# A hybrid layer's scan: decays and their scaling placed first in each projection tile

## The chip, the cores and the metric

The kernel runs on one core of one Trainium2 chip. The metric is the device time of one execution in microseconds (us). Three runs of the kernel before gave 2807.34 to 2811.86 us, with a median of 2810.05 us.

## The reference, cut to what matters

Two transformer-like blocks run one after the other on 512 tokens of width 1024. The first block has a state-space scan, a windowed attention and a mixture of experts; the second has attention and dense feed-forward layers. The change touches only the scan of the first block and what shares its time:

```python
z, xbc, dt_raw, q, k, v, g_ssd, g_att = jnp.split(h @ w_in, IN_SPLITS, axis=-1)
...
a_cum = jnp.cumsum(dt_c * a.reshape(G, J), axis=2)            # G=4 groups, J=8 heads, chunks of L=128
seg = a_cum[:, :, :, None] - a_cum[:, :, None, :]
decay = jnp.exp(jnp.where(causal, seg, -jnp.inf))
cb = jnp.einsum('bclgn,bcsgn->bclsg', cm, bm)
y_diag = jnp.einsum('bclsgj,bcsgjp->bclgjp', cb[..., None] * decay, xdt)
states = jnp.einsum('bclgn,bclgjp->bcgjpn', bm, xdt * decay_to_end[..., None])
...                                                            # carried over the 4 chunks
y_off = jnp.einsum('bclgn,bcgjpn->bclgjp', cm, prev) * jnp.exp(a_cum)[..., None]
y = y_diag + y_off + xs * d_skip
...
q = partial_rope(rms_norm(q, q_norm_g), cos, sin)              # the same for k; v is only projected
```

Everything is float32; the large products split each operand in a high and a low part and use three matmuls.

## The kernel before, in words

Each stage of the kernel has one function for each engine (`qkv_pe`, `qkv_act`, `qkv_dve`, `qkv_pool`, `qkv_sp`, and `mix_*` in the same way). A function lists its engine's instructions in program order. An engine takes them strictly in that order, and they wait for one another across engines by semaphores. So where a call stands in such a function decides behind which waits it sits.

**The stage qkv** is a loop over 14 tiles t: two of k, eight of q (each 128 columns of the weights, 24 matmuls of 512 columns on TensorE, "dense") and four of v (24 matmuls of 256 columns). For the q and k tiles ScalarE copies and squares the product (L1035, L1036), TensorE sums the squares of tile t-1 (L1025, "blk"), ScalarE makes the root from them (L1044, L1046), VectorE scales (L1066, "normed"). Then comes the rotation of tile t-2: TensorE (L1019, "rot"), VectorE times the sine (L1058), GpSimd times the cosine (L1082), VectorE adds them (L1061). VectorE copies the v tiles (L1070). Weight pieces are split ahead of use, the high part on ScalarE (`piece_hi`, L415) and the low part on VectorE (`piece_lo`, L429).

**The scan** has 16 units i, one for each of 4 groups and 4 chunks c (c = i mod 4). Unit i is laid beside tile t = i + 4 (`S_FIRST` = 4), the later ones beside the rounds of the next stage. For one unit:

- `decay_sp`: SyncE loads the unit's 512 KB of cumulated decays, broadcast from DRAM, in one of two buffers (the ring `EX`, L842). The load of unit i waits until the products of unit i-2 have left the buffer.
- `decay_act`: ScalarE, in place, eight Relu instructions (L888) and one Exp over 1024 columns (L890).
- `cb_pe`, `cb_dve`: TensorE makes C·B (L849), VectorE masks it (L897).
- `weights_dve`: VectorE multiplies the 1024 columns of decays by it (L903, "weights").
- `scan_pool`: GpSimd makes x·dt (L941, "xd"), x·dt·decay-to-end (L947, "xe") and x·D (L948, "skip").
- `scan_pe`: TensorE multiplies weights and xd (L861, 16 matmul records, "ydiag"), the old state (L871, "yoff", not for c = 0) and the new state (L879, "state", not for c = 3).
- `scan_dve`: VectorE adds them to y and carries the state (L911 to L933).

In tile t the products of unit t-5 run on TensorE, behind the tile's dense. On VectorE the weights of unit t-5 stand at the head of tile t, behind the piece; on ScalarE the decays of unit t-4 stand at the end of tile t, behind the norms of tile t-1.

**The stage mix** walks one list, `MIX`, on all engines: 19 rounds r, in each the scan step "s0" of unit r+10 (decays, C·B) and "s1" of unit r+9 (the products), four attention steps ("a2", "a1", "b0", "a0"), two z tiles ("z": 24 matmuls of 256 columns, ScalarE tanh L1229, VectorE L1273, GpSimd L1294), and the weight pieces of z ("w"). The scan is through after round 6. In mix the weights of unit r+9 are the first thing of "s0" on VectorE, behind the z steps of the round before. The raw z pieces have a single buffer, so that the load of a piece waits until the piece ahead is split.

Of the kernel before, what the change touches and what calls it, by code (L numbers as in the profile page):

```python
# [220 lines left out]
def build(nc, d, out):  # L221
    ctx = ExitStack()
    with ctx:
# [753 lines left out]

        def qkv_pe(e):
            for t in range(14):
                if 1 < t < 10:  # L980
                    qkv_dense(e, t)
                elif t >= 10:
# [12 lines left out]
                    m.then_inc(*(WS1.of(ns[0]).free(K.pe, "mm", t) if t == 13 else K.pe.up("mm", t)))  # L995
                    if t == 13:
                        WS1.of(ns[1]).frees.update(WS1.of(ns[0]).frees)
                if t == S_FIRST:
                    e.wait_ge(*X.act.to("turned", 19))
                    e.wait_ge(*D.act.to("done"))  # L1000
                if t >= S_FIRST:
                    cb_pe(e, t - S_FIRST)
                if t > S_FIRST:
                    scan_pe(e, t - 1 - S_FIRST)
                if 0 <= t - 4 < 2:
# [21 lines left out]
        def qkv_act(e):  # L1027
            for t in range(14):
                piece_hi(e, qkv_ahead(t))
                if t < 10:  # L1030
                    b, q = BR.of("qkv", t), HBQ.take(t)
                    for s, n in q.before:
                        e.wait_ge(s, n)
                    e.wait_ge(*K.pe.to("mm", t))
                    e.activation(qkv_out(t), b.ap[:, :], ACT.Copy).then_inc(*K.act.up("cp", t))  # L1035
                    e.activation(q.ap, b.ap[:, :], ACT.Square).then_inc(*b.free(K.act, "sq", t))  # L1036
                if 0 <= t - 4 < 2:
                    b = BR.of("swap", t - 4)
                    e.wait_ge(*K.pe.to("swap", t - 4))
                    e.activation(KT[:, 2 * (t - 4) + 1, :], b.ap[:, :], ACT.Copy).then_inc(*b.free(K.act, "swap", t - 4))  # L1040
                if 0 <= t - 1 < 10:
                    b, q = BR.of("blk", t - 1), HBQ.of(t - 1)
                    e.wait_ge(*K.pe.to("blk", t - 1))
                    e.activation(q.ap, b.ap[:, :], ACT.Ln, bias=C["eps"]).then_inc(*b.free(K.act))  # L1044
                    e.wait_ge(*K.act.now())
                    e.activation(q.ap, q.ap, ACT.Exp, scale=-0.5).then_inc(*K.act.up("rs", t - 1))  # L1046
                if t >= S_FIRST:
                    decay_act(e, t - S_FIRST)

        def qkv_dve(e):  # L1050
            for t in range(14):
                piece_lo(e, qkv_ahead(t), False)
                if t > S_FIRST:
                    weights_dve(e, t - 1 - S_FIRST)
                if 0 <= t - 2 < 10:
                    b, x, q = BR.of("rot", t - 2), qkv_out(t - 2), HBQ.of(t - 2)
                    e.wait_ge(*K.pe.to("rot", t - 2))
# [9 lines left out]
                if t >= 10:  # L1067
                    b = BR.of("qkv", t)
                    e.wait_ge(*K.pe.to("mm", t))
                    e.tensor_copy(VT[:, t - 10, :], b.ap[:, 0:256]).then_inc(*b.free(K.dve, "v", t))  # L1070
                if t >= S_FIRST:
                    cb_dve(e, t - S_FIRST)
                if t > S_FIRST:
                    scan_dve(e, t - 1 - S_FIRST)

        def qkv_pool(e):
            e.wait_ge(*L.act.to("cos"))
# [28 lines left out]
        for r in range(19):  # L1106
            first = [j // 4 for j in Z_ROUNDS[r] if j % 4 == 0]
            MIX += [("w", AT["z", a, 1]) for a in first]
            MIX += [(f, r + S_BESIDE - lag) for f, lag in (("s0", 0), ("s1", 1)) if r + S_BESIDE - lag < 16]
            MIX += [(f, r - lag) for f, lag in (("a2", 3), ("a1", 2), ("b0", 1), ("a0", 0)) if 0 <= r - lag < 16]  # L1110
            MIX += [("z", j) for j in Z_ROUNDS[r]]
            MIX += [("w", AT["z", a, 1] + 1) for a in first]

# [117 lines left out]
        def mix_dve(e):  # L1231
            for what, i in MIX:
                if what == "s0":
                    weights_dve(e, i - 1)
                    cb_dve(e, i)
                if what == "s1":
                    if i == 15:
                        weights_dve(e, i)
                    scan_dve(e, i)
                if what == "a0":  # L1240
                    n_, kv = ATT_UNITS[i]
                    w = 256 if n_ else 128
# [2359 lines left out]
```

## Time and profile before

| | |
|---|---|
| median of three runs | 2810.05 us |
| the profiled execution | 2808.63 us, with a span of 2806.8 us |
| span outside its first and last instruction | 1.83 us |
| TensorE busy in the whole span | 92% |
| tiles 5 to 13 of qkv, up to the last ydiag | 214.5 to 354.3 us |
| rounds 0 to 6 of mix (the rest of the scan) | 354.3 to 484.0 us |

The span is what the profile's rows are counted in. Busy TensorE is not TensorE at its peak: its clock has two levels, 2.4 and 1.2 GHz, and a row of a stretch gives the granted share as PEclk.

### The profile page before, as it was taken

Reading aid. Unit: us, or ns where it says so; the run is one execution under the profiler, and the core shown is the slowest. Engines: PE = TensorE matmul, PEld = TensorE weight load, DVE = VectorE, ACT = ScalarE, POOL = GpSimd, SP = SyncE. Lnnn points to the kernel's source line nnn. Section 1 sums busy time; section 2 is a strip of 40 time slices with the busy share of each in tenths; the row PEclk is TensorE's granted clock in tenths of the full one; section 3 lists DMA queues with packets and bytes.
Section 4 is the critical chain, followed back from the end, with each engine's and each line's share of the span. In section 5 each row is a group of like instructions: output and inputs, shape, how many; then the busy total and the mean of one; then the engine's idle time right before and its main releaser. Section 6 shows DMA issues by size and latency. Waiting matters only on the chain.

```text
span 2806.8 us, 41459 instructions
## 1 busy us (share of the span) xinstructions
PE 2585.2 (92%) x16510; PEld 2114.5 (75%) x16510; DVE 1145.8 (41%) x2009; ACT 1055.8 (38%) x2157; POOL 826.5 (29%) x538
## 2 busy tenths in 40 slices
PE   7998778999997888888999998999999999999999
PEld 6875556888875555555798878999999887777877
DVE  7754444533124111111435664134257776512212
ACT  4444343553222211112435564323324555532231
POOL 1002343422331032200221103655541111465553
PEclk9998778999998999999999999999999999999999
DMA  4231121233328999999331111233332111233332
GB/s 144 83 86 45 43 70 46 61 106 83 99 71 321 409 426 426 426 426 419 138 106 50 57 31 53 83 91 98 91 87 76 49 46 46 60 90 91 105 91 67
DMA packets 328417, 378.78 MB, mean 135 GB/s; under 512 B 10480, under 2 KB 300400, under 8 KB 303648
## 3 DMA queue, kind: packets, MB, share of 16 engines
q1 hardware_dynamic: 327072, 371.91, 38.3%
q0 software_dynamic: 1152, 4.19, 0.4%
q8 instruction: 134, 2.20, 0.3%
q14 instruction: 59, 0.48, 0.1%
HBM read 371.81 MB, written 4.26 MB: 134 GB/s over the span
## 4 chain that ended last, share of the span: by engine, by line
PE 64%; DMA 12%; DVE 9%; issue 6%; ACT 5%; POOL 5%; SPq 0%; ACTq 0%; DVEq 0%; POOLq 0%
DMA early<-in_w_up_e 11%; PE bank L2478 5%; PE bank L2480 5%; PE bank L2479 5%; PE bank L1972 5%; PE bank L2985 4%; PE bank L2986 4%; PE bank L2987 4%; PE bank L443 3%; PE bank L444 3%; PE bank L445 3%; POOL split L2453 2%; DVE early L684 2%; PE bank L861 1%; PE bank L1186 1%
## 5 line engine op out<-in xcount | busy, mean ns | idle before, releaser
L2453 POOL TENSOR_TENSOR split<-keep,split 128x1024 fp32r<-128x1024 f32 x143 | 348.8, 2443 | 453.0 <-ACT split L2427 453.0
L2478 PE MATMUL bank<-x_hi,split 128*128 128x264 f32 (+1 forms) x1280 | 397.6, 311 | 11.1 <-POOL split L2453 9.3
L2480 PE MATMUL bank<-x_hi,split 128*128 128x264 f32 (+1 forms) x1280 | 390.6, 305 | 0.0
L2479 PE MATMUL bank<-x_lo,split 128*128 128x264 f32 (+1 forms) x1280 | 390.4, 305 | 0.0
L2427 ACT ACTIVATE split<-keep 128x1024 fp32r<-128x1024 f32 x192 | 200.2, 1050 | 222.8 <-PE bank L2987 208.0
L1972 PE MATMUL bank<-early 128*64 128x256 f32 x2048 | 236.5, 384 | 40.0 <-DMA early<-in_w_up_e 32.1
L2478 PEld LDWEIGHTS bank<-x_hi,split 128*128 128x128 f32 x1280 | 241.4, 189 | 32.3 <-issue 19.8
L1972 PEld LDWEIGHTS bank<-early 128*64 128x64 f32 x2048 | 165.7, 138 | 122.0 <-issue 72.4
L2479 PEld LDWEIGHTS bank<-x_lo,split 128*128 128x128 f32 x1280 | 241.6, 189 | 10.1 <-issue 0.2
L2480 PEld LDWEIGHTS bank<-x_hi,split 128*128 128x128 f32 x1280 | 240.6, 188 | 10.4
L3023 DVE TENSOR_TENSOR mlp<-mlp,bank 128x264 f32<-128x264 f32 (+1 forms) x96 | 49.5, 515 | 326.7 <-ACT mlp L3002 326.7
L2985 PE MATMUL bank<-hidden0h,split 128*128 128x264 f32 x512 | 145.5, 284 | 1.1 <-issue 1.1
L415 ACT ACTIVATE w_split<-early 128x1024 fp32r<-128x1024 f32 (+1 forms) x101 | 105.6, 1047 | 106.3 <-PE bank L445 97.0
L2986 PE MATMUL bank<-hidden0l,split 128*128 128x264 f32 x512 | 145.0, 283 | 0.0
L2987 PE MATMUL bank<-hidden0h,split 128*128 128x264 f32 x512 | 145.0, 283 | 0.0
L2090 DVE TENSOR_TENSOR early<-early,bank 128x256 f32<-128x256 f32 x32 | 13.5, 421 | 314.9 <-PE bank L2013 198.1
L1996 PE MATMUL bank<-early 128*64 128x512 f32 x512 | 116.9, 598 | 21.5 <-DVE early L2097 21.5
L3033 DVE TENSOR_TENSOR mlp<-bank,roots 128x264 f32<-128x264 f32 (+1 forms) x96 | 46.9, 516 | 206.1 <-PE bank L2987 206.1
L429 DVE TENSOR_TENSOR w_split<-early,w_split 128x1024 fp32r<-128x1024 f32 (+1 forms) x70 | 87.4, 1248 | 103.6 <-ACT w_split L415 103.6
L443 PE MATMUL bank<-x_hi,w_split 128*128 128x512 f32 x304 | 123.6, 407 | 1.0 <-DVE w_split L429 0.4
L3002 ACT ACTIVATE mlp<-bank 128x264 f32<-128x264 f32 (+1 forms) x96 | 43.5, 453 | 202.7 <-PE bank L2480 202.7
L445 PE MATMUL bank<-x_hi,w_split 128*128 128x512 f32 x304 | 119.1, 392 | 0.0
(490 smaller groups left out, 6132.9 us busy)
## 6 DMA issues: line engine op xcount, KB each, us to landing
early<-in_w_gate_e SPq DMA_DIRECT2D x64, 1024.0 KB, 11.2
early<-in_w_up_e SPq DMA_DIRECT2D x64, 1024.0 KB, 11.4
early<-in_w_down_e SPq DMA_DIRECT2D x64, 1024.0 KB, 10.7
early<-in_w_in SPq DMA_DIRECT2D x68, 512.0 KB, 3.7
keep<-in_mlp_w_in SPq DMA_DIRECT2D x64, 512.0 KB, 3.9
keep<-in_mlp_w_out SPq DMA_DIRECT2D x64, 512.0 KB, 3.7
keep<-in_a_w_qkv SPq DMA_DIRECT2D x24, 512.0 KB, 4.6
early<-decay_rows SPq DMA_DIRECT2D x16, 512.0 KB, 5.8
```

The costliest lines, as they stand in the source:

```text
L443: e.matmul(o, hi[:, k, :], xh, start=first and k == 0, stop=False, skip_group_check=True)
L445: m = e.matmul(o, lo[:, k, :], xh, start=False, stop=last and k == 7, skip_group_check=True)
L1972: m = e.matmul(b.ap[cols(j, 64), o:o + 256], x.ap[:, k, cols(j, 64)], wtile(us[j], 8, 256)[:, k, :], start=k == 0, stop=k == 7, skip_group ...
L1996: m = e.matmul(b.ap[cols(j, 64), :], ht.ap[:, f * 128 + 64 * j:f * 128 + 64 * j + 64], wtile(us[j], 2, 1024)[:, f, cols(q, 512)], start=f ...
L2427: e.activation(hi, x, ACT.Copy).then_inc(*S.act.up("hi", n))
L2453: e.tensor_tensor(lo, x, whole(hi), ALU.subtract).then_inc(*u.free(sig_, "lo", n))
L2478: e.matmul(o, hi[:, k, :], xh, start=k == 0, stop=False, skip_group_check=True)
L2479: e.matmul(o, hi[:, k, :], xl, start=False, stop=False, skip_group_check=True)
L2480: m = e.matmul(o, lo[:, k, :], xh, start=False, stop=k == 7, skip_group_check=True)
L2985: e.matmul(o, hi[:, k, :], yh[:, k, n0 - at:n1 - at], start=k == 0, stop=False, skip_group_check=True)
L2986: e.matmul(o, hi[:, k, :], yl[:, k, n0 - at:n1 - at], start=False, stop=False, skip_group_check=True)
L2987: m = e.matmul(o, lo[:, k, :], yh[:, k, n0 - at:n1 - at], start=False, stop=k == 7, skip_group_check=True)
```

## The change: what it does

In the stage qkv, TensorE's C·B of unit t-4 moves from behind the dense of tile t ahead of it. ScalarE's decays of unit t-4 move from the end of tile t to behind its weight piece, ahead of the copy, the square and the root. On VectorE tile t now does, behind its weight piece, the mask and the weights of unit t-4 and then the additions of unit t-5, all ahead of rotation, norm and v copy; before, it did the weights of unit t-5 there, and mask and additions at the end. So weights are made in the tile ahead of their products. The stage mix gets an entry "sw": the weights of unit r+10 stand in round r behind "a0" and ahead of "z", where before they stood in round r+1 behind the z steps of round r and that round's first piece. No instruction is added or removed, and no load or buffer is changed.

```diff
--- before.py
+++ after.py
@@ -977,6 +977,11 @@
 
         def qkv_pe(e):
             for t in range(14):
+                if t == S_FIRST:
+                    e.wait_ge(*X.act.to("turned", 19))
+                    e.wait_ge(*D.act.to("done"))
+                if t >= S_FIRST:
+                    cb_pe(e, t - S_FIRST)
                 if 1 < t < 10:
                     qkv_dense(e, t)
                 elif t >= 10:
@@ -995,11 +1000,6 @@
                     m.then_inc(*(WS1.of(ns[0]).free(K.pe, "mm", t) if t == 13 else K.pe.up("mm", t)))
                     if t == 13:
                         WS1.of(ns[1]).frees.update(WS1.of(ns[0]).frees)
-                if t == S_FIRST:
-                    e.wait_ge(*X.act.to("turned", 19))
-                    e.wait_ge(*D.act.to("done"))
-                if t >= S_FIRST:
-                    cb_pe(e, t - S_FIRST)
                 if t > S_FIRST:
                     scan_pe(e, t - 1 - S_FIRST)
                 if 0 <= t - 4 < 2:
@@ -1027,6 +1027,8 @@
         def qkv_act(e):
             for t in range(14):
                 piece_hi(e, qkv_ahead(t))
+                if t >= S_FIRST:
+                    decay_act(e, t - S_FIRST)
                 if t < 10:
                     b, q = BR.of("qkv", t), HBQ.take(t)
                     for s, n in q.before:
@@ -1044,14 +1046,15 @@
                     e.activation(q.ap, b.ap[:, :], ACT.Ln, bias=C["eps"]).then_inc(*b.free(K.act))
                     e.wait_ge(*K.act.now())
                     e.activation(q.ap, q.ap, ACT.Exp, scale=-0.5).then_inc(*K.act.up("rs", t - 1))
-                if t >= S_FIRST:
-                    decay_act(e, t - S_FIRST)
 
         def qkv_dve(e):
             for t in range(14):
                 piece_lo(e, qkv_ahead(t), False)
+                if t >= S_FIRST:
+                    cb_dve(e, t - S_FIRST)
+                    weights_dve(e, t - S_FIRST)
                 if t > S_FIRST:
-                    weights_dve(e, t - 1 - S_FIRST)
+                    scan_dve(e, t - 1 - S_FIRST)
                 if 0 <= t - 2 < 10:
                     b, x, q = BR.of("rot", t - 2), qkv_out(t - 2), HBQ.of(t - 2)
                     e.wait_ge(*K.pe.to("rot", t - 2))
@@ -1068,10 +1071,6 @@
                     b = BR.of("qkv", t)
                     e.wait_ge(*K.pe.to("mm", t))
                     e.tensor_copy(VT[:, t - 10, :], b.ap[:, 0:256]).then_inc(*b.free(K.dve, "v", t))
-                if t >= S_FIRST:
-                    cb_dve(e, t - S_FIRST)
-                if t > S_FIRST:
-                    scan_dve(e, t - 1 - S_FIRST)
 
         def qkv_pool(e):
             e.wait_ge(*L.act.to("cos"))
@@ -1108,6 +1107,7 @@
             MIX += [("w", AT["z", a, 1]) for a in first]
             MIX += [(f, r + S_BESIDE - lag) for f, lag in (("s0", 0), ("s1", 1)) if r + S_BESIDE - lag < 16]
             MIX += [(f, r - lag) for f, lag in (("a2", 3), ("a1", 2), ("b0", 1), ("a0", 0)) if 0 <= r - lag < 16]
+            MIX += [("sw", r + S_BESIDE)] if r + S_BESIDE < 16 else []
             MIX += [("z", j) for j in Z_ROUNDS[r]]
             MIX += [("w", AT["z", a, 1] + 1) for a in first]
 
@@ -1231,12 +1231,11 @@
         def mix_dve(e):
             for what, i in MIX:
                 if what == "s0":
-                    weights_dve(e, i - 1)
                     cb_dve(e, i)
                 if what == "s1":
-                    if i == 15:
-                        weights_dve(e, i)
                     scan_dve(e, i)
+                if what == "sw":
+                    weights_dve(e, i)
                 if what == "a0":
                     n_, kv = ATT_UNITS[i]
                     w = 256 if n_ else 128
```

VectorE in the stage qkv, the kernel before, at one tile with c = 1 or 2 (L1058 is the sine product of rotation and so the first instruction behind the weights of unit t-5):

```order
L903 TENSOR_TENSOR early<-early 128x1024
L1058 TENSOR_TENSOR early<-bank,early 128x512
L1061 TENSOR_TENSOR early<-early 128x512
L1066 SCALAR_TENSOR_TENSOR early<-early,lasting 128x512
L897 TENSOR_TENSOR early<-bank,lasting 128x128
L911 TENSOR_TENSOR early<-early,bank 128x512
L917 TENSOR_TENSOR ints<-bank,early 128x512
L919 TENSOR_TENSOR early<-early,ints 128x512
L930 TENSOR_TENSOR early<-early 128x512
L933 TENSOR_TENSOR early<-early,bank 128x512
L429 TENSOR_TENSOR w_split<-early,w_split 128x1024
L903 TENSOR_TENSOR early<-early 128x1024
```

VectorE at the same place in the kernel of the change, whose lines L1061, L1064 and L1069 are L1058, L1061 and L1066 of before:

```order
L429 TENSOR_TENSOR w_split<-early,w_split 128x1024
L897 TENSOR_TENSOR early<-bank,lasting 128x128
L903 TENSOR_TENSOR early<-early 128x1024
L911 TENSOR_TENSOR early<-early,bank 128x512
L917 TENSOR_TENSOR ints<-bank,early 128x512
L919 TENSOR_TENSOR early<-early,ints 128x512
L930 TENSOR_TENSOR early<-early 128x512
L933 TENSOR_TENSOR early<-early,bank 128x512
L1061 TENSOR_TENSOR early<-bank,early 128x512
L1064 TENSOR_TENSOR early<-early 128x512
L1069 SCALAR_TENSOR_TENSOR early<-early,lasting 128x512
```

L903 now follows L897 of its own unit directly and stands ahead of the additions of the unit before; the rotation comes last.

ScalarE in the stage qkv, the kernel before, tiles of q (L1035 and L1036 copy and square, L1044 and L1046 make the root, L415 is the weight piece of the next tile):

```order
L1035 ACTIVATE early<-bank 128x512
L1036 ACTIVATE early<-bank 128x512
L1044 ACTIVATE early<-bank,lasting 128x512
L1046 ACTIVATE early<-early 128x512
L888 ACTIVATE early<-early 128x128 x8
L890 ACTIVATE early<-early 128x1024
L415 ACTIVATE w_split<-early 128x1024
```

ScalarE there in the kernel of the change, with L1037, L1038, L1046 and L1048 for the four lines:

```order
L415 ACTIVATE w_split<-early 128x1024
L888 ACTIVATE early<-early 128x128 x8
L890 ACTIVATE early<-early 128x1024
L1037 ACTIVATE early<-bank 128x512
L1038 ACTIVATE early<-bank 128x512
L1046 ACTIVATE early<-bank,lasting 128x512
L1048 ACTIVATE early<-early 128x512
```

The decays L888 and L890, which wait for their load, now stand ahead of the copy and the square, which wait for the dense.

VectorE in round 1 of mix, the kernel before (L1250 to L1263 are the attention step "a0", L1273 the two z steps, L903 the weights of the unit whose products run in the next round):

```order
L1250 SCALAR_TENSOR_TENSOR early<-bank,lasting 128x256 x2
L1254 TENSOR_REDUCE early<-early 128x4
L1260 TENSOR_TENSOR early<-early,lasting 128x4
L1262 TENSOR_TENSOR early<-lasting,early 128x4
L1263 TENSOR_SCALAR early<-early 128x4
L1273 SCALAR_TENSOR_TENSOR early<-early,bank 128x256 x2
L429 TENSOR_TENSOR w_split<-early,w_split 128x1024
L903 TENSOR_TENSOR early<-early 128x1024
```

The same in the kernel of the change (every line number but L903 and L429 is one less):

```order
L1249 SCALAR_TENSOR_TENSOR early<-bank,lasting 128x256 x2
L1253 TENSOR_REDUCE early<-early 128x4
L1259 TENSOR_TENSOR early<-early,lasting 128x4
L1261 TENSOR_TENSOR early<-lasting,early 128x4
L1262 TENSOR_SCALAR early<-early 128x4
L903 TENSOR_TENSOR early<-early 128x1024
L1272 SCALAR_TENSOR_TENSOR early<-early,bank 128x256 x2
L429 TENSOR_TENSOR w_split<-early,w_split 128x1024
```

L903 no longer stands behind the z steps and the weight piece.

## Rows read from the trace of the kernel before

**Rows 1.** Waits, 207 to 490 us: waiting, releaser, us in total, times, longest.

```profile
PE bank L861 <- DVE early L903: 54.8, 14, 11.7
```

**Rows 2.** Windows by stretch; columns as in the first row.

```profile
core 0: us, PE busy (x) PEld busy (x) DVE busy (x) ACT busy (x) POOL busy (x), PEclk, DMA share, GB/s
214.50:354.30 139.80, 108.32 (x435) 79.03 (x433) 66.03 (x81) 52.84 (x118) 40.99 (x33) 0.77 0.18 46
354.30:380.90 26.60, 14.91 (x83) 11.61 (x82) 9.56 (x17) 9.51 (x25) 9.41 (x8) 0.68 0.30 79
380.90:484.00 103.10, 85.60 (x504) 67.85 (x502) 49.38 (x97) 43.41 (x127) 39.03 (x33) 0.80 0.19 52
484.00:493.10 9.10, 9.10 (x75) 7.90 (x76) 4.06 (x11) 5.13 (x15) 5.65 (x4) 1.00 0.20 59
```

**Rows 3.** Timeline of PE, tile 7: start, duration, instruction, idle before and releaser.

```profile
248.87 0.79 PE L443 MATMUL bank<-x_hi,w_split 128*128 128x512 f32 x1
...
254.76 0.38 PE L849 MATMUL bank<-early 128*128 128x128 f32 x2
259.51 3.65 PE L861 MATMUL bank<-early 128*128 128x64 f32 x16 [4.37 <-DVE early L903]
...
267.18 0.80 PE L443 MATMUL bank<-x_hi,w_split 128*128 128x512 f32 x1
```

**Rows 4.** Timeline of PE, tile 3, which has no scan, and tile 13.

```profile
198.63 0.79 PE L443 MATMUL bank<-x_hi,w_split 128*128 128x512 f32 x1
...
204.52 1.02 PE L1019 MATMUL bank<-early,lasting 128*128 128x512 f32 x2
205.38 1.02 PE L1025 MATMUL bank<-early,lasting 128*128 128x512 f32 x2
205.83 0.79 PE L443 MATMUL bank<-x_hi,w_split 128*128 128x512 f32 x1
...
352.53 1.90 PE L861 MATMUL bank<-early 128*128 128x64 f32 x16
```

**Rows 5.** Timeline of DVE, tile 3 (first row) and tile 7.

```profile
207.75 0.69 DVE L1061 TENSOR_TENSOR early<-early 128x512 f32<-128x512 f32 x1 [1.48 <-POOL early L1082]
...
248.62 0.69 DVE L1058 TENSOR_TENSOR early<-bank,early 128x512 f32<-128x512 f32 x1 [8.09 <-PE bank L1019]
250.79 1.45 DVE L1061 TENSOR_TENSOR early<-early 128x512 f32<-128x512 f32 x1 [1.48 <-POOL early L1082]
252.16 1.53 DVE L1066 SCALAR_TENSOR_TENSOR early<-early,lasting 128x512 f32<-128x512 f32 x1
...
257.05 1.22 DVE L429 TENSOR_TENSOR w_split<-early,w_split 128x1024 fp32r<-128x1024 f32 x1
258.19 1.22 DVE L903 TENSOR_TENSOR early<-early 128x1024 f32<-128x1024 f32 x1
```

**Rows 6.** Timeline of ACT, tile 7: the decays of one unit.

```profile
250.74 2.44 ACT L888 ACTIVATE early<-early 128x128 f32<-128x128 f32 x8
253.21 1.06 ACT L890 ACTIVATE early<-early 128x1024 f32<-128x1024 f32 x1
```

**Rows 7.** All 16 decay loads, issue to landing.

```profile
DMA to landing us min/median/max: 5.5/5.8/8.1
```

**Rows 8.** Timeline of POOL: xd in tile 7.

```profile
250.65 1.03 POOL L941 TENSOR_TENSOR early<-early 128x512 f32<-128x512 f32 x1
```

**Rows 9.** Timeline, start of mix: POOL's z piece, DVE's z piece, z tiles on PE.

```profile
357.69 2.34 POOL L429 TENSOR_TENSOR w_split<-early,w_split 128x1024 fp32r<-128x1024 f32 x1
...
364.79 1.23 DVE L429 TENSOR_TENSOR w_split<-early,w_split 128x1024 fp32r<-128x1024 f32 x1 [8.62 <-ACT w_split L415]
...
375.03 0.39 PE L1186 MATMUL bank<-w_split,x_hi 128*128 128x256 f32 x1
...
380.89 0.39 PE L849 MATMUL bank<-early 128*128 128x128 f32 x2
```

**Rows 10.** Waits of SyncE's queue, 780 to 900 us.

```profile
SPq L1891 <- DVE lasting L1467: 40.5, 1, 40.5
```

## The prediction

> **What bounds the kernel now.** I read the waits between engines first, because busy shares say nothing about order. From 207 to 490 us TensorE waits 14 times, 54.8 us in all, and always with the same pair: the products of a scan unit (L861) wait for VectorE's weights (L903) [rows 1]. The windows then show how wide the matter is. From tile 5 to the last ydiag beside a projection tile pass 139.8 us, and up to the end of the scan another 26.6 and 103.1 us. TensorE has 60.7 us there with no matmul at all (139.8 - 108.3, 26.6 - 14.9 and 103.1 - 85.6 give 31.5 + 11.7 + 17.5), and its granted clock is 0.77, 0.68 and 0.80. In a round of mix without the scan it is busy all the time, at 1.00 [rows 2]. The other engines are busy at most half of these stretches [rows 2], so nothing but the order of work can hold TensorE up.
>
> The timeline of tile 7 shows the order. Its period is 267.18 - 248.87 = 18.3 us. Dense ends and C·B starts at 254.76; ydiag starts only at 259.51, 4.37 us idle, and then takes 3.65 us [rows 3], against 1.90 us in tile 13, where nothing had stalled [rows 4]. So a stall is paid twice: once as the wait, and once because TensorE then runs at its lower level, 1.2 GHz, for what follows. The tile before the scan begins shows the unstalled price: dense, rot and blk in 205.83 - 198.63 = 7.20 us [rows 4].
>
> VectorE's timeline of the same tile says why the weights are late. It runs without a pause from the sine at 248.62 to the end of the weights at 258.19 + 1.22 = 259.4, but for 1.48 us in which GpSimd multiplies the cosine. That is 10.8 us [rows 5]. It starts only when TensorE has done rot, and dense, beside which it runs, takes less than 6 us (204.52 - 198.63) [rows 4]. The weights stand last in this chain although their inputs have long been there: ScalarE's decays ended at 253.21 + 1.06 = 254.3 [rows 6].
>
> **The change, part by part.** No instruction comes or goes, so the sum is one of waits.
>
> *Stage qkv, TensorE alone.* A 512-column float32 product costs 205.38 - 204.52 = 0.86 us at full clock [rows 4], C·B about 0.3 [rows 3] and ydiag 1.9 [rows 4]. A tile with c = 1 or 2 then costs 7.20 + 0.3 + 1.9 + 2 x 0.86 = 11.1 us, one with c = 0 or 3 (no yoff, or no state) 10.3. A v tile is shorter by 24 x (0.227 - 0.122) = 2.5 us; the 0.122 is half a z pair over 24, (380.89 - 375.03)/48 [rows 9], the 0.227 is (204.52 - 198.63 - 0.43)/24 [rows 4], where 0.43 is my reading of the start. Tiles 5 to 9 (tile 5 has the 0.86 of a swap instead of yoff): 3 x 11.1 + 2 x 10.3 = 53.9. Tile 10: 8.6; tile 11, with no blk, 7.7; tile 12, with no rot and c = 3, 6.5; tile 13 up to the end of ydiag 5.6. Sum 82.3 us, against 139.8.
>
> *What the new order makes it wait for.* Let T be the end of the ydiag of unit i-2. The decay load of unit i is issued then and lands 5.8 us later, 8.1 at worst [rows 7]. ScalarE takes 2.44 + 1.06, some 3.5 us [rows 6], and VectorE 1.2 for the weights [rows 5]: T + 10.5. Behind that now stand the additions of unit i-1 (from 253.6 to 257.05, 3.4 us), the sine (0.7), GpSimd's cosine (1.5) [rows 5] and xd (1.03) [rows 8], which ydiag of unit i needs: T + 17.2, and ydiag ends at T + 19.1. That is two tiles, so 9.6 us a tile: less than TensorE's 11.1, and TensorE does not wait. VectorE's own tile stays 10.8 us long [rows 5], also below 11.1. Moving ScalarE's decays ahead of copy and square costs them T + 9.3, about when dense ends (T + 9.2), and what needs the square stands a tile later; I take 0. With the load at 8.1 us the chain gives 10.7 a tile: still 0. C·B ahead of dense waits for a bank that the mask of the unit before frees a tile earlier; its worth is 0.
>
> In the v tiles TensorE's 7 to 8 us fall below the chain's 9.6. Tiles 11 and 12 then stall some 2 to 3 us each and pay the lower clock: I take 6 us for both together, with 0 and 12 as bounds. Stage qkv: 82.3 + 6 = 88, so **-52 us**.
>
> A rule of the Trainium skill speaks against the move. What the rows show is this: VectorE's addition of two SBUF operands takes 0.69 us with GpSimd idle and 1.45 us with GpSimd running its scan operations [rows 5]. The Trainium skill, page "SBUF — State Buffer", section "Who interferes with whom", says that a VectorE instruction with two SBUF inputs and a GpSimd one that reads SBUF lock each other out, whichever comes second waiting. By that rule, the trace agrees, the piece and the weights can each be lengthened when GpSimd's skip overlaps them; by the rule at its worst the sum would be smaller by 1.2 us in each of nine tiles. By the rows alone a doubled L903 would make VectorE's tile 12.0 us, 0.9 over TensorE's; I take 0 and keep nine times 0.9 = 8 us for the range.
>
> *Start of mix.* Let E be the end of the last ydiag, 354.3 now. z tile 0 starts at 375.03, E + 20.7. It stood behind the products of unit 9, whose weights stood behind the z piece that VectorE ended at 364.79 + 1.23 = 366.0, E + 11.7. That piece hangs on the single raw buffer, which GpSimd frees at 357.69 + 2.34 [rows 9], and the change does not touch it. Weights 9 now stand ahead of it, so the products run while the piece is awaited and z starts at about E + 11.8: -8.9 us. It starts after an idle stretch, so I add 3.5 us for a z pair partly at the lower clock (an estimate: 5.86 us at full clock [rows 9], 11.7 if all of it were at half, and somewhat over the middle of the two). Together **-5.4 us**.
>
> *Rounds 1 to 6 of mix.* Now 103.1 us, 17.2 each [rows 2]. A round without the scan takes 9.1 us at full clock and with the whole attention [rows 2]; the scan adds 0.3 + 1.9 + 1.7 = 3.9. A z pair and the scan alone give 9.8; all of it 13.0. The attention joins step by step in these rounds, so I take 11.1, 67 us; bounds 59 and 78. In VectorE's list the weights now fill the time in which it waited for ScalarE's exp and tanh. So **-36 us**, bounds -44 and -25.
>
> *After the scan* nothing changes, and the gain has to survive. The next place where loads bound the kernel is the experts' weights; their first load waits 40.5 us in SyncE's queue for a VectorE instruction of the stage before [rows 10]. So it starts with the compute and moves with it: the gain is kept.
>
> Sum: 52 + 5.4 + 36 = 93 us. The profiled execution took 2808.6 us, 1.4 below the median of the runs; 2808.6 - 93 = 2715.6, on the median's scale 2717. The sum lets every stall be gone to the last tenth; I give back 3 us for that: **2720 us**.
>
> **The rivals.**
> *A, the stall gets shorter but stays* (chance 0.22). What speaks for it: VectorE's 10.8 and TensorE's 11.1 us are close, and after each longer wait the clock falls. If in each of 15 tiles and rounds about 1.5 us of wait and 1.5 us of lower clock remain, 45 us are lost: 2765 us. Against it: the same stretch shows waits to be harmful above all when VectorE's whole chain stands between rot and ydiag [rows 3, 5], and that chain is cut.
> *B, the gain is absorbed later* (0.03). If the expert loads bounded the time from an issue that does not move, all but some us would be lost, and the time would be 2800 to 2810. [Rows 10] speak against it.
> *C, slower* (0.04). The decays now stand ahead of the copy on ScalarE, and their load is issued only after a ydiag. If the load comes so late that the square is not there a tile later, blk waits, the root and the norm with it, and then rot, and ydiag behind them. From T the square has to be done by the blk of the next tile, about T + 20; load, decays and copy give T + 10.5 [rows 6, 7]. It decides from a landing of 15 us on. For a loss against before, a tile must be above 17 us, so the landing must be at 22 us; at 24 us it would be 2 us a tile over 9 tiles, 2830 us. The slowest of 16 took 8.1 us [rows 7].
> *The forecast* has 0.71.
>
> A rule of the Trainium skill bears on rival A. First the row: after 4.37 us idle ydiag runs at the lower level, 3.65 instead of 1.90 us [rows 3, 4]. The page "TensorE: Matmul & The Clock Gate", section "Part 1: The HAM clock gate (the "warmup" mystery)", describes the same two levels, with the lower one as the state after idleness.
>
> **How the numbers follow.** The bounds of the forecast are 0 or 12 us for the v tiles, up to 8 us in the q tiles, 59 to 78 in the rounds, and none of the 3 us given back: 2720 - 6 - 8 - 3 = 2703 to 2720 + 6 + 8 + 11 = 2745 us. Rival A adds the part up to its 2765. Leaving out its upper half, B and C, about 2 in 10, the range is 2700 to 2757. A measurement of this kernel can tell 0.2%, 5.6 us, from no change. The forecast, A and most of what lies between give faster 0.94; half of B same, 0.02; C and the unknown slower 0.04.
>
> **What the profile after would show.** The waits of L861 for L903 are gone or below 10 us. TensorE's period is 11 us in tiles 6 to 9, and ydiag takes 1.9 us there. PEclk is near 1.00 up to tile 10. The v tiles 11 and 12 show ydiag waiting for GpSimd's xd. z tile 0 starts some 12 us after the last ydiag beside a tile. Rounds 1 to 6 take 10 to 13 us, and a round without the scan 9.1 as before. I am wrong if the rotation, now last on VectorE, makes rot or xd the new wait in every tile, or if the clock stays low with short waits.

## The result and the profile after

| | before | changed |
|---|---|---|
| median, side by side | 2809.81 us | 2717.55 us (2715.61 to 2721.07, 4 runs) |
| ratio, 95% interval | | 0.9673 [0.9657, 0.9690] |
| profiled execution, its span | 2808.63, 2806.8 us | 2717.27, 2715.5 us |
| granted clock of TensorE, whole span | 0.967 | 0.985 |

The forecast was 2720 us, range 2700 to 2757. Two single runs further on, one of 3172 us in experiment 3 and one of 3599 us with the first edit of experiment 4, lie far above the others of their kernels, with a granted clock of 0.75 and 0.65, and are left out of the ratios.

I read the profile after in the order of the views before. First TensorE's waits from 200 to 410 us (which engine and line it waited for, us in total, times, longest):

```profile
PE bank L849 <- DVE early L1073: 7.4, 1, 7.4
PE bank L861 <- POOL early L941: 4.2, 2, 3.4
PE bank L1186 <- ACT early L1222: 1.2, 2, 1.0
PE bank L861 <- DVE early L903: 1.1, 2, 0.6
```

The 54.8 us in which the products L861 waited for the weights L903 [rows 1] have become 1.1. At the top stands a wait that I had not foreseen, of C·B (L849) for VectorE's copy of a v tile (L1073).

The windows of the changed kernel, with the stretches cut at the same instructions as before (columns as in [rows 2]):

```profile
core 0: us, PE busy (x) PEld busy (x) DVE busy (x) ACT busy (x) POOL busy (x), PEclk, DMA share, GB/s
215.10:302.50 87.40, 83.24 (x434) 64.00 (x432) 67.83 (x78) 48.49 (x103) 41.80 (x33) 0.96 0.29 73
302.50:324.20 21.70, 14.34 (x82) 11.60 (x81) 13.06 (x18) 11.10 (x30) 9.26 (x7) 0.76 0.44 97
324.20:393.40 69.20, 66.94 (x502) 56.56 (x500) 56.47 (x96) 41.88 (x127) 40.92 (x34) 1.00 0.29 77
393.40:402.50 9.10, 9.10 (x75) 7.86 (x74) 4.80 (x10) 5.22 (x18) 5.62 (x4) 1.00 0.19 59
```

Set against [rows 2]: 139.8 has become 87.4 (-52.4), 26.6 has become 21.7 (-4.9), and 103.1 has become 69.2 (-33.9). Together that is 91.2 us, and the spans differ by 2806.8 - 2715.5 = 91.3. The whole gain lies in these three stretches. The round without the scan takes 9.1 us, as before.

The same rows tell the two ways in which a stall was paid. TensorE's time without a matmul in the three stretches falls from 60.7 us to 13.8 (178.3 - 164.5), by 46.9. Its busy time falls from 208.8 us to 164.5, by 44.3, with the same products to make: that is the clock, since PEclk went from 0.77, 0.68 and 0.80 to 0.96, 0.76 and 1.00. So nearly half of the gain is clock and not waiting.

TensorE's timeline shows what a tile looks like now (start, duration, instruction, idle before in brackets). Tiles 7 and 8, then the products of tiles 10 to 12, then the start of mix:

```profile
237.27 0.39 PE L849 MATMUL bank<-early 128*128 128x128 f32 x2
242.99 1.89 PE L861 MATMUL bank<-early 128*128 128x64 f32 x16
...
248.21 0.38 PE L849 MATMUL bank<-early 128*128 128x128 f32 x2
...
271.56 1.97 PE L861 MATMUL bank<-early 128*128 128x64 f32 x16
...
283.49 3.65 PE L861 MATMUL bank<-early 128*128 128x64 f32 x16 [3.38 <-POOL early L941]
...
294.92 1.97 PE L861 MATMUL bank<-early 128*128 128x64 f32 x16 [0.78 <-POOL early L941]
...
310.91 0.80 PE L849 MATMUL bank<-early 128*128 128x128 f32 x2 [7.36 <-DVE early L1073]
311.50 3.52 PE L861 MATMUL bank<-early 128*128 128x64 f32 x16
314.80 2.02 PE L871 MATMUL bank<-early 128*128 128x512 f32 x2
...
318.36 0.39 PE L1186 MATMUL bank<-w_split,x_hi 128*128 128x256 f32 x1
```

The period of a q tile is 248.21 - 237.27 = 10.94 us, where it was 18.3, and ydiag takes 1.89 us with no wait, where it took 3.65 after a wait of 4.37 [rows 3]. In v tile 11 it waits 3.38 us for GpSimd's xd and runs at the lower clock; in tile 12 it waits 0.78 and keeps the full one. The first z tile starts 15.9 us after the last ydiag (302.5), not 11.8.

VectorE's timeline at the end of the stage says why. The first row is the weights made in tile 12, the others belong to tile 13:

```profile
296.28 1.23 DVE L903 TENSOR_TENSOR early<-early 128x1024 f32<-128x1024 f32 x1 [0.42 <-ACT early L890]
...
306.31 3.02 DVE L903 TENSOR_TENSOR early<-early 128x1024 f32<-128x1024 f32 x1 [5.64 <-ACT early L890]
309.25 0.67 DVE L911 TENSOR_TENSOR early<-early,bank 128x512 f32<-128x512 f32 x1
309.85 0.68 DVE L926 COPY early<-bank 128x512 f32<-128x512 f32 x1
310.45 0.41 DVE L1073 COPY early<-bank 128x256 f32<-128x256 f32 x1
```

and ScalarE's and GpSimd's rows of the same moment:

```profile
302.67 2.45 ACT L888 ACTIVATE early<-early 128x128 f32<-128x128 f32 x8 [6.50 <-DMA early<-decay_rows]
305.15 1.06 ACT L890 ACTIVATE early<-early 128x1024 f32<-128x1024 f32 x1
```

```profile
305.91 2.34 POOL L429 TENSOR_TENSOR w_split<-early,w_split 128x1024 fp32r<-128x1024 f32 x1
```

Unit 9's decays land only at 302.67, since their load is issued at the end of ydiag 7 (296.9). The weights wait for them, and the copy of v tile 13 now stands behind the weights. The function of TensorE in mix begins with a wait for just that copy. So C·B of unit 10, the products of unit 9 and z all wait. The weights themselves take 3.02 us instead of 1.23, beside GpSimd's z piece. And after the wait of 7.36 us the products of unit 9 run at the lower clock, 3.52 us for ydiag and 2.02 for yoff, before z has its turn.

### The profile page after: what moved, and what is told of

The parts are those of the page before. It is cut to its first block, busy times and chain, and to the rows that moved or that the text cites. A ratio compares the mean times of both kernels' runs of the same rounds, so it can differ in the third digit from the quotient of the medians.

```text
span 2715.5 us, 41459 instructions
## 1 busy us (share of the span) xinstructions
PE 2542.4 (94%) x16510; PEld 2089.7 (77%) x16510; DVE 1140.9 (42%) x2009; ACT 1055.7 (39%) x2157; POOL 831.1 (31%) x538
## 4 chain that ended last, share of the span: by engine, by line
PE 69%; DMA 12%; DVE 7%; ACT 5%; POOL 4%; issue 3%; SPq 0%; ACTq 0%; DVEq 0%; POOLq 0%
DMA early<-in_w_up_e 11%; PE bank L2477 5%; PE bank L2478 5%; PE bank L2479 5%; PE bank L1971 5%; PE bank L443 5%; PE bank L444 5%; PE bank L445 5%; PE bank L2984 4%; PE bank L2985 4%; PE bank L2986 4%; POOL split L2452 2%; PE bank L3254 1%; PE bank L2730 1%; PE bank L1186 1%
## 5 line engine op out<-in xcount | busy, mean ns | idle before, releaser
L415 ACT ACTIVATE w_split<-early 128x1024 fp32r<-128x1024 f32 (+1 forms) x101 | 105.7, 1047 | 104.4 <-PE bank L445 97.0
L429 DVE TENSOR_TENSOR w_split<-early,w_split 128x1024 fp32r<-128x1024 f32 (+1 forms) x70 | 91.8, 1312 | 95.4 <-ACT w_split L415 95.4
## 6 DMA issues: line engine op xcount, KB each, us to landing
early<-in_w_gate_e SPq DMA_DIRECT2D x64, 1024.0 KB, 10.9
early<-in_w_up_e SPq DMA_DIRECT2D x64, 1024.0 KB, 11.8
```

## The experiments

The runs came in four jobs, each with runs of the kernel before beside it; ratios are to those, each with its 95% interval. "Changed" is the changed kernel.

### 1. The two halves alone

The kernel before with the part in mix only:

```
 MIX += [... "a2", "a1", "b0", "a0" ...]
+MIX += [("sw", r + S_BESIDE)] if r + S_BESIDE < 16 else []
 MIX += [("z", j) for j in Z_ROUNDS[r]]
 # mix_dve
 if what == "s0":
-    weights_dve(e, i - 1)
+    if i == S_BESIDE: weights_dve(e, i - 1)
     cb_dve(e, i)
 if what == "s1":
-    if i == 15: weights_dve(e, i)
     scan_dve(e, i)
+if what == "sw": weights_dve(e, i)
```

> The kernel before with the change in the stage mix alone: the weights of unit r+10 behind a0 and ahead of the z steps (the weights of unit 9 still behind the first z piece). Theory (two independent parts that add up): the six rounds give back their 34 us, 103 to about 69, the projection tiles stay at 139.8 us, z tile 0 starts as before at 20.7 us after the last ydiag: 2810 - 34 = 2776 us. Rival (what the rounds gain hangs on the tiles being early too): less than 20 us, over 2790.

And the reverse, the changed kernel with mix as before from unit 10 on:

> The changed kernel with mix as before from unit 10 on: the weights of a unit stand at the head of the next round again, behind its z piece. Theory (the parts add up): tiles 87.4 us instead of 139.8, start of mix -5, rounds 1 to 6 stay at 103 us: 2810 - 57 = 2753 us. Rival (the parts share one gain): both parts alone give more than their share, and this one comes under 2740.

Measured: 2776.26 us, 0.9883 [0.9866, 0.9900], and 2751.81 us, 0.9803 [0.9786, 0.9819]. Against 2809.75 in the same job that is -33.5 and -57.9 us, together 91.4, where the whole change gave 92.3. The halves add up, so neither lives on the other. The waits of TensorE from 207 to 490 us with mix alone:

```profile
PE bank L861 <- DVE early L903: 38.8, 10, 11.8
```

### 2. ScalarE's move without VectorE's, and VectorE's without ScalarE's

The kernel before with only this edit:

```
 # qkv_act
 piece_hi(e, qkv_ahead(t))
+if t >= S_FIRST:
+    decay_act(e, t - S_FIRST)
 ...
-if t >= S_FIRST:
-    decay_act(e, t - S_FIRST)
```

> The kernel before with ScalarE's decays moved alone (behind the weight piece, ahead of copy, square and root); VectorE, TensorE and mix as before. Theory (what holds TensorE is where VectorE's weights stand, last behind rotation, norm and additions; the decays had long been ready): 2810 us, within 6 us. Rival (the decays' place is a good part of the gain): 2790 or less. A third outcome, slower by 10 us or more, would say that decays ahead of the copy cost something that the new VectorE order hides.

Measured: 2807.71 us (10 runs), 0.9994 [0.9984, 1.0003]: nothing. Then the reverse, the changed kernel with this edit taken back:

> The changed kernel with ScalarE's decays put back to the end of their tile, behind the root; the new VectorE order and mix stay. Theory: weights of unit i, first on VectorE in tile t, now wait for decays that start only behind the root of tile t-1, and additions, sine, cosine and xd stand behind them. From the ydiag of unit i-2 (T): root ends T + 15.7, decays T + 19.2, weights T + 20.5, xd T + 27.5, so the next ydiag ends at T + 29 for two units' distance, 14.6 us a tile instead of 11. Nine tiles give +30 us: 2748 us, and TensorE's waits are for xd, not for the weights. Rival (ScalarE's order does not matter): 2718 us.

Measured: 2783.17 us, 0.9913 [0.9897, 0.9930]. That missed my 2748 by 35 us. Waits of TensorE, then of VectorE, from 205 to 420 us:

```profile
PE bank L861 <- POOL early L941: 45.1, 8, 9.4
PE bank L849 <- DVE early L1073: 7.4, 1, 7.4
```

```profile
DVE early L903 <- ACT early L890: 75.9, 9, 11.2
```

TensorE's timeline of one tile of it:

```profile
233.33 0.38 PE L849 MATMUL bank<-early 128*128 128x128 f32 x2
243.92 3.65 PE L861 MATMUL bank<-early 128*128 128x64 f32 x16 [4.72 <-POOL early L941]
253.25 0.38 PE L849 MATMUL bank<-early 128*128 128x128 f32 x2
```

A tile takes 19.9 us, longer than the 18.3 of before. I had reckoned that blk, root, decays, weights, additions, sine, cosine and xd form a loop over two tiles. It is a loop over one: the xd at its end is waited for by the ydiag of the very next tile, and blk stands right behind that ydiag on TensorE. So ScalarE's move is worth nothing alone (2 us, within its interval), but VectorE's order needs it: without it VectorE's head waits 75.9 us for decays that stand behind a root that is not ready, and 65.6 of the 92 us are lost. Of the 26.6 us that remain the part in mix gives 33.5 by experiment 1, so outside the rounds VectorE's order by itself would cost some 7 us (33.5 - 26.6). The trace agrees: from tile 5 to the last ydiag pass 149.6 us where it was 139.8, so the tiles lose 9.8 us, and the start of mix gives some of it back.

### 3. C·B ahead of dense or behind it

The changed kernel with `cb_pe` back behind the dense products:

```
 # qkv_pe
-if t >= S_FIRST: cb_pe(e, t - S_FIRST)
 ... dense ...
+if t >= S_FIRST: cb_pe(e, t - S_FIRST)
 if t > S_FIRST:
     scan_pe(e, t - 1 - S_FIRST)
```

> The changed kernel with TensorE's C·B of unit t-4 put back behind the dense of tile t. Theory (the mask and the weights wait for the decays anyway, which end when dense ends): 0, within 4 us of the changed kernel's 2717.5. Rival (C·B ahead of dense is what lets the mask go first on VectorE): VectorE waits about 6 us a tile for C·B with the additions behind it, 2740 or more.

Measured: 2720.33 us, 0.9684 [0.9671, 0.9696]. The intervals of this ratio and the changed kernel's overlap: no effect that can be told. So the third part of the change is worth nothing that these runs can show, as its cost of 0 had it.

### 4. The wait that was missed, and xd

Three edits of the changed kernel. The first puts GpSimd's scan work ahead of the cosine, from the second scan tile on:

```
 # qkv_pool
+if t > S_FIRST:
+    scan_pool(e, t - S_FIRST)
 if t < 12:
     ... x * COS ...
-if t >= S_FIRST:
+if t == S_FIRST:
     scan_pool(e, t - S_FIRST)
```

> The changed kernel with GpSimd's scan work of unit t-4 ahead of the cosine of tile t-2 in every tile from 5 on. Theory (what is left of TensorE's wait in the v tiles, 3.4 and 0.8 us for xd and the lower clock behind, comes from xd standing behind additions, sine and cosine): both waits go, 7 us less: 2710. In the q tiles nothing changes, because TensorE did not wait there. Rival (the scan work then collides with VectorE's additions or makes the cosine late): 2718 or more.

The second moves TensorE's wait for the copy of v tile 13 to the place where the copy is read:

```
 # mix_pe
-e.wait_ge(*K.dve.to("v", 13))
+e.wait_ge(*K.dve.to("rotated", 9))
 for what, i in MIX:
+    if what == "a2" and i == 0:
+        e.wait_ge(*K.dve.to("v", 13))
```

> The changed kernel with TensorE's wait for the last v copy moved from the head of mix to the first product that reads v (the head waits for the last rotation instead). Theory (the 7.4 us wait at C·B of unit 10 hides a second one, the weights of unit 9, which end 1.5 us ahead of the v copy): z tile 0 starts 1 to 2 us earlier: 2716. Rival (the wait is a cost of its own): 7 us less, 2710.

Measured: 2716.66 us, 0.9672 [0.9660, 0.9685] with the first, and 2718.95 us, 0.9682 [0.9669, 0.9694] with the second. Neither differs from the changed kernel by more than can be told. The traces tell more. With the first no wait for xd is left (waits of TensorE, 200 to 410 us):

```profile
PE bank L849 <- DVE early L1073: 5.1, 1, 5.1
PE bank L1019 <- DVE early L1073: 2.5, 1, 2.5
PE bank L861 <- DVE early L903: 2.0, 4, 0.7
```

and z tile 0 starts at 311.17 instead of 318.36, 7.2 us earlier. But the first expert load is issued at 752.5 us against 758.8, the last at 1243.2 against 1246.8, and the spans are 2715.0 and 2715.5. Of 7.2 us, 6.3 reach the experts, 3.6 come out of them, and 0.5 the end. With the second the wait for the copy is gone, and the one that stood behind it has come out:

```profile
PE bank L861 <- DVE early L903: 6.7, 3, 5.7
```

z tile 0 starts at 317.00, only 1.4 us earlier. So what holds the start of mix is the chain behind both, the late decay load and the weights. The copy was merely its last link.

The next kernel has both, and GpSimd's z piece, which frees the raw buffer for VectorE's, moves from mix into tile 12, so that it ends at 298.0 instead of 308.3 us:

```
 # qkv_pool
 if t > S_FIRST:
     scan_pool(e, t - S_FIRST)
+if t == 12:
+    piece_lo(e, Z_FIRST, True)
```

With it in the same job ran the first edit alone and the changed kernel, both again:

> The changed kernel with three more moves: GpSimd's scan work ahead of the cosine, TensorE's wait for the last v copy at the first product that reads v, and GpSimd's low part of the first z piece in tile 12 instead of at the head of mix. Theory: the first takes 7 us from the stage, the second 1 to 2, the third lets VectorE's weights of unit 9 run beside no GpSimd work (they took 3.02 us beside it, 1.22 alone) and brings z tile 0 2 to 3 us forward. The expert loads start 10 us earlier than in the changed kernel. If this stands to the end: 2708 us. Rival (the stages behind give part of it back, as after the move of GpSimd's scan work, where 6.3 us at the expert loads became 1 us at the end): 2712 to 2717.

> The kernel with GpSimd's scan work ahead of the cosine once more, beside the changed kernel on one chip. If the 6.3 us that its profile shows at the first expert load are lost to nothing but the spread between executions, its median is 4 to 7 us under that of the changed kernel; if something behind absorbs them, the medians are within 2 us.

> The changed kernel once more, on the chip of the next three, so that differences of a few us can be read side by side: 2717.5 us, within 2.

| | median (range) | ratio | z tile 0 starts | first expert load |
|---|---|---|---|---|
| changed, again | 2720.47 (2716.58 to 2723.66) | 0.9694 [0.9681, 0.9708] | 317.90 | 758.4 |
| GpSimd's scan first, again | 2716.12 (2713.67 to 2721.94) | 0.9681 [0.9667, 0.9695] | 315.25 | 755.5 |
| all three | 2712.48 (2707.66 to 2718.62) | 0.9674 [0.9660, 0.9689] | 308.89 | 750.4 |

TensorE's timeline with all three: the products of units 8 and 9, and z tile 0.

```profile
294.88 1.97 PE L861 MATMUL bank<-early 128*128 128x64 f32 x16 [0.28 <-DVE early L903]
...
301.81 3.65 PE L861 MATMUL bank<-early 128*128 128x64 f32 x16 [3.83 <-DVE early L903]
...
308.89 0.38 PE L1192 MATMUL bank<-w_split,x_hi 128*128 128x256 f32 x1
```

z tile 0 stands 12.1 us behind the last ydiag beside a tile (296.8), near the 11.8 that the prediction had for the changed kernel, but not by its path: the products of unit 9 still wait 3.83 us for their weights, and ydiag takes 3.65 us behind that wait. The first expert load comes 8.0 us earlier than in the changed kernel, and the median is 8.0 us lower. This is the fastest of the versions. But its interval touches the changed kernel's, and its own five runs spread over 11 us: by the times it is about 0.3% better, and not surely so. z tile 0 of the first edit alone stands at 311.17 in the one job and 315.25 in the other, so single traces of the start of mix differ by 4 us, and a step of that size is not to be read from one.

### 5. How near VectorE is to the bound

Each q and k tile's sine product is made three times, then seven times; only the last one is used. That adds 2 x 0.7 = 1.4 and 6 x 0.7 = 4.2 us of VectorE's time to each of ten tiles, 14 and 42 us in all:

```
 # qkv_dve
+for _ in range(2):          # 6
+    e.tensor_tensor(q.ap, b.ap[:, :], SIN, ALU.mult)...
 e.tensor_tensor(q.ap, b.ap[:, :], SIN, ALU.mult)...
```

> The changed kernel with the sine product of each of the ten rotated tiles made three times (the same result), so that VectorE's chain in a tile is 1.4 us longer. Theory (VectorE's 10.3 to 10.8 us a tile are just under TensorE's 10.9, short waits do not lower TensorE's clock): the tile becomes VectorE's, about 11.8 us, +1 us in each of eight tiles and 1.4 us each in tiles 10 and 11: 2728 us, PEclk in tiles 6 to 9 near 1.00. Rival A of the prediction (waits of 1 to 2 us lower the clock): the waits come with ydiag and yoff at half clock, +4 us a tile, 2750 or more.

> The changed kernel with the sine product of each of the ten rotated tiles made seven times, so that VectorE's chain in a tile is 4.2 us longer. The tile is VectorE's then: 10.3 + 4.2 = 14.5 us, 3.5 over TensorE's 11. Theory without the clock: 8 tiles of +3.5 and two v tiles of +4.2 give +36, 2754 us. The question is whether TensorE's clock falls in waits of 3 to 4 us: if it does, ydiag takes 3.65 us instead of 1.9, but because VectorE sets the period this costs nothing more, unless the chain through ydiag is the longest; then 2770 or more.

Measured: 2730.81 us, 0.9720 [0.9708, 0.9733], and 2757.69 us, 0.9832 [0.9817, 0.9848], beside 2720.47 for the changed kernel in the second's job. TensorE's products with three sines:

```profile
243.64 1.97 PE L861 MATMUL bank<-early 128*128 128x64 f32 x16 [0.34 <-POOL early L941]
...
256.74 1.97 PE L861 MATMUL bank<-early 128*128 128x64 f32 x16 [1.96 <-POOL early L941]
...
267.68 1.97 PE L861 MATMUL bank<-early 128*128 128x64 f32 x16 [0.67 <-POOL early L941]
```

and with seven:

```profile
240.55 1.97 PE L861 MATMUL bank<-early 128*128 128x64 f32 x16 [1.04 <-POOL early L941]
...
256.54 3.63 PE L861 MATMUL bank<-early 128*128 128x64 f32 x16 [4.81 <-POOL early L941]
...
272.54 2.66 PE L861 MATMUL bank<-early 128*128 128x64 f32 x16 [1.52 <-POOL early L941]
...
286.37 2.83 PE L861 MATMUL bank<-early 128*128 128x64 f32 x16 [1.88 <-POOL early L941]
```

With seven, TensorE waits 23.4 us for xd, in 8 places from 200 to 410 us. VectorE from 215 to 302 us is never held up but by the cosine and once by rot:

```profile
DVE early L1067 <- POOL early L1084: 8.7, 6, 1.5
DVE early L1062 <- PE bank L1019: 1.8, 1, 1.8
```

The 42 us of added work cost 37, in one job with the changed kernel. The 14 us cost 7 to 13: 13 against its first ratio (0.9720 - 0.9673 of 2809), 7 against its second, 0.9694, since it did not run in that job. From three sines to seven 28 us more cost 27 (31 by the ratios). In the traces TensorE's four tiles from the C·B of tile 6 to that of tile 10 take 45.6 us with three sines (226.51 to 272.12) and 42.0 in the changed kernel (226.36 to 268.33), 3.6 us more for 5.6 us of sines. So the changed kernel has only a small lead over VectorE to use up, and beyond it VectorE sets the pace almost one for one. The rival's view, that every short wait also brings the lower clock, is wrong for these q tiles with three sines, which run at full clock. It is partly right for seven, where ydiag takes 2.66 to 3.63 us. Yet the time stays near the sum without it. VectorE's rows suggest why: it hardly waits for TensorE, whose slower matmuls then mostly fill its own idle time.

## Why the prediction came out right

**The bound.** TensorE was held by the order of work: the weights stood behind the rotation, the norm and the additions. The waits, the windows, and experiments 1 and 2 all say so. Shown.

**Stage qkv, 82.3 + 6 = 88 us:** measured 87.4. The period is 10.9 us with c = 1 or 2 (worked out: 11.1), 1.89 for ydiag, PEclk 0.96 over the stretch. Tiles 5 to 9 take 53.2 us (53.9), tile 10 8.5 (8.6) and tile 11 14.0 (7.7 without a stall). Tiles 12 and 13 were added up wrongly: by the prediction's own terms they are 6.0 and 5.1 us, not 6.5 and 5.6. They took 6.75, of which 0.78 is a wait, and 4.9. So the sum was 1 us too high, and the stalls of tiles 11 and 12 cost 7.1 us (6.3 + 0.75) and not 6. With tiles 5 to 9 0.7 us shorter than reckoned, the errors nearly cancel.

One step failed, though the sum did not feel it: that VectorE's own tile stays 10.8 us long, below TensorE's 11.1. VectorE's sine products of tiles 5, 7 and 9:

```profile
225.70 0.69 DVE L1061 TENSOR_TENSOR early<-bank,early 128x512 f32<-128x512 f32 x1 [1.37 <-PE bank L1019]
...
249.24 0.69 DVE L1061 TENSOR_TENSOR early<-bank,early 128x512 f32<-128x512 f32 x1
...
268.37 0.68 DVE L1061 TENSOR_TENSOR early<-bank,early 128x512 f32<-128x512 f32 x1
```

The two tiles of c = 1 and 2 take 23.5 us from sine to sine (225.70 to 249.24), 11.8 each against TensorE's 10.9, and the two of c = 3 and 0 take 19.1, 9.6 each against TensorE's 10.1. The four together are 42.7 us on VectorE and 42.0 on TensorE: VectorE is a little slower, and not faster. What keeps TensorE from waiting is a lead. The xd that ydiag needs ends 3.3 us ahead of it in tile 6, 1.6 us in tile 8 (252.30 against 253.92) and 0.15 us in tile 10 (271.41 against 271.56). That this lead lasted through the q tiles was in part luck.

**The chain of two tiles, 9.6 us a tile.** It was enough not to be seen in the q tiles, and it showed in v tile 11 with 3.38 us and in tile 12 with 0.78, in both for xd, as foreseen. From the end of ydiag 4 (T = 265.9) the xd of unit 6 ends at 283.3, T + 17.5, where T + 17.2 was worked out. The 6 us for both tiles were an estimate, inside whose bounds of 0 and 12 the 7.1 lie, but the shares were not 2 to 3 each and a clock: nearly all fell in tile 11, and tile 12 paid no lower clock. The chain's length with the decays elsewhere I counted wrong (experiment 2). There the step that failed was the count of tiles in the loop, and it had no part in the forecast.

**VectorE beside GpSimd.** I took 0 for the lengthening and kept 8 us for the range. The lengthening is there, as these rows of VectorE and GpSimd in tile 7 show:

```profile
242.54 2.06 DVE L429 TENSOR_TENSOR w_split<-early,w_split 128x1024 fp32r<-128x1024 f32 x1
```

```profile
242.03 1.49 POOL L948 TENSOR_TENSOR early<-early,lasting 128x512 f32<-128x512 f32 x1
```

The piece takes 2.06 us beside the skip, against 1.22 before [rows 5]. It does so in tiles 5, 6, 7 and 9, and this is the main reason why VectorE's tiles of c = 1 and 2 are longer than 10.8 us. The shorter tiles that follow make most of it good, and the lead of the xd covers the rest, so TensorE waits for none of it in the q tiles: 0 was right in time, with little to spare. Where nothing makes it good, it costs: the weights of tile 13 take 3.02 us. The Trainium skill, page "SBUF — State Buffer", section "Who interferes with whom", has a VectorE instruction with two SBUF inputs and a GpSimd one that reads SBUF lock each other out. By that rule, the trace agrees, with 3.02 instead of 1.23 us beside GpSimd's 2.34.

**Start of mix, -5.4 us:** measured -4.9, by two errors that cancel. z tile 0 comes 15.9 us behind the last ydiag, not 11.8. The step failed that weights 9 run while the piece is awaited: they wait for the decay load, take 3.02 us, and hold the v copy for which TensorE waits. I had costed the moved v copy at nothing without asking who waits for it first. Against that stand the 3.5 us which I added for a z pair at the lower clock. The z pair takes 324.2 - 318.36 = 5.85 us, as at full clock [rows 9]. So -8.9 + 4.1 = -4.8, with no term for z. The lower clock was not absent, it fell on the products of unit 9 ahead of z: C·B 0.80 us where it is 0.39 at full clock, ydiag 3.52 where it is 1.90, yoff 2.02 where it is 1.08. That is some 3 us (an estimate from these rows) of the 4.1. The term was about the right size at the wrong instructions, and that the sum came out is luck. With all three edits of experiment 4 z comes at 12.1, again behind products at the lower clock.

**Rounds 1 to 6, -36 us:** measured -33.9. Their 69.2 us are 11.5 a round against my 11.1. The term was too large by 2.1 us, inside its bounds.

**After the scan, nothing lost.** SyncE's queue from 690 to 810 us:

```profile
SPq L1890 <- DVE lasting L1466: 40.5, 1, 40.5
```

The same 40.5 us as in [rows 10], with the load 849.1 - 758.8 = 90.3 us earlier. The gain is carried whole to the end. Small gains are not always: in the traces the first edit of experiment 4 lost most of its 7 us behind this point, while all three together kept their 8. What eats them I have not settled.

**The 3 us given back.** The sum itself, 2717 on the median's scale, was nearer to 2717.55 than the 2720. Mix came out 2.1 + 0.5 us worse than its terms, qkv 0.4 better.

**The rivals.** A, the stall stays and with it the lower clock: did not occur, since the waits are 5.3 us in 4 places for L861. B, absorbed later: refuted by the 91.2 us before and 91.3 us at the end. C, slower through late decay loads: all landed within 8.4 us. But ScalarE does wait 19.8 us for them in 7 places, so this is the next thing to become late.

## What to carry to other kernels

When an engine takes its list in order, look for an operation whose inputs are ready long before its turn, and ask who waits for its result. Put it ahead of the chain that isn't urgent, and move its producer too: here, in the projection tiles, ScalarE's move alone gave nothing and VectorE's alone a loss of some 7 us, and both together 58 of gain. And for each instruction that thereby stands later, look up its first waiter, also in the next stage. A copy costed at nothing held the start of mix here. Before counting on a loop's length, follow it until it returns to the same instruction and count the tiles that it spans.

## What the runs showed of the hardware beyond that

Short waits of TensorE do not all lower its clock. After 0.34, 0.67, 0.78, 1.04 and 1.96 us the next products took 1.97 us, at full clock. After 1.52, 1.88, 3.38, 3.83, 4.72 and 4.81 us they took 2.66 to 3.65, in part or wholly at the lower one. The two sets overlap (1.96 stayed full, 1.52 did not, 16 us after one of 4.81), so the length of the one wait doesn't decide alone. Which other thing does, these runs don't settle.

A VectorE product of 128x1024 float32 beside a GpSimd one of the same size (the weights beside the z piece, which itself took 2.34 us) took 3.02 and 2.78 us in two executions of the changed kernel. The weights of tiles 5 to 9, with GpSimd idle, took 1.22 to 1.23. Where the weights came first, in tile 12 (296.28), they took 1.23, and GpSimd's xd that began 0.7 us into them took 1.43 instead of 1.04.
